# RMS factors of the MLP: a row in every partition by two transfers through DRAM, in place of four transposes and two copies

## The chip, the cores and the metric

One core of one Trainium2 chip runs the whole kernel. The metric is the device time of one execution in microseconds (us). The kernel before took 762.76 us (median of three runs, 762.75 to 763.80).

## The reference, cut to what matters

A decoder layer on 512 tokens of 1024 channels: a gated convolution and a sliding-window attention are merged and added to the residual `x`; then a squared-ReLU MLP; all float32. The change touches the first RMS norm of the MLP alone:

```python
def rmsnorm(x, g):
    y = x * lax.rsqrt(jnp.mean(x * x, axis=-1, keepdims=True) + EPS)
    return y * g
...
h2 = rmsnorm(x, mlp_norm_g)                                  # (512, 1024)
x = x + jnp.square(jax.nn.relu(h2 @ w_up)) @ w_down          # w_up (1024, 4096), w_down (4096, 1024)
return rmsnorm(x, final_norm_g)
```

The factor of a token is one positive number, so the kernel multiplies with it only after `w_up` and the ReLU: `relu(a * f) = relu(a) * f`.

## The kernel before, in words

There is no planner: each of the five engines has its own program, written out in the order in which it is to run, and the programs meet at semaphores. A wait stops everything behind it on its engine.

Twelve products of 1024 x 1024 weights follow each other as stages s = 0 to 11. Stages 0 to 3 belong to the mixers, and 4 to 11 are the MLP: an even stage multiplies with a quarter of `w_up`, the odd one after it with the same quarter of `w_down`. Each stage is done by a scheme of seven half-size products with sums of blocks (M1, N2, M6, M5, M7, M3, N4, in this order), and each of these in three passes over a high and a low part of both operands ("kinds" 0, 1 and 2 in `up_product`, L818, and `product`, L856). ACT rounds the high parts (`high_part` L1150 for weights, `s_high` L1166 and `h2_high` L1288 for activations); DVE subtracts to make the low parts (`low_part` L1694, `s_low` L1701, `h2_low` L1764) and does the sums. Weights come by the queues of SP (blocks, L485) and POOL (sums of blocks accumulated by the transfer: "T3" at L605, "T1" at L610 and L614).

In an even stage the output has channels in partitions and tokens along the free axis. So a token's factor must stand in every partition, as the row `rrow` [128, 512]. `relu(4, 0)` (L1859, instruction L1868) is the first to read it; fifteen later ones read it too.

How the row is made before: ACT's `square_part` (L1298) sums squares of the residual into `ss2`; DVE's `token_sums` (L1781) adds two halves; ACT takes the square root (L1359, after `high_part(4, M5)`); DVE's `token_factors` (L1785) takes the reciprocal into `rr2[:, 1, :]`, a factor a token, tokens in partitions, and copies it (L1789) to 128 columns each in `rbc`; PE transposes the four blocks of `rbc` (L809) into PSUM bank 7, between kind 0 and kind 1 of product M5 of stage 4; ACT copies the bank to `rrow` (L1368) after `copy_out(4, zc12, M6)`.

Behind `relu(4, 0)` on DVE stand `h2_low` of M3 and N4, `s_low(5, M1)`, `sum_t2(5)`, `low_part(4, M3)`, and on to stage 5. `square(4, 0)` on ACT (L1309) waits for `relu(4, 0)`, and behind it stand `s_high(5, M1)`, `high_part(4, M3)` and `copy_out(4, zc22, M5)` (L1202). Product M3 of stage 4 on PE waits for that copy (`copied`, L953).

Of the kernel before, what the change touches and what calls it, by code (L numbers as in the profile page):

```python
# [7 lines left out]
F32 = mybir.dt.float32  # L8
F32R = mybir.dt.float32r
ALU = mybir.AluOpType  # L10
ACT = mybir.ActivationFunctionType

P = 128
D = 1024
T = 512
KT = D // P
TB = T // P
# [20 lines left out]
M1, N2, M6, M5, M7, M3, N4 = range(7)  # L38
# [139 lines left out]
def build(nc, x, attn_norm_g, w_in, conv_w, w_conv_out, attn_sinks, rel_bias, w_attn_out, w_o,  # L178
          mlp_norm_g, w_up, w_down, final_norm_g, out):
    ctx = ExitStack()  # L180
    with ctx:
# [4 lines left out]
        def place(name, shape, dt=F32, offset=None):  # L186

            size = 4 * int(np.prod(shape[1:]))
            if offset is None:
                offset = top[0]  # L190
                top[0] = -(-(offset + size) // 64) * 64
            return nc.alloc_sbuf_tensor_at(name, shape, dt, offset=offset)
# [44 lines left out]
        tz = place("tz", [P, 2, T + 2])  # L237
        ty_at = top[0]
        ty = place("ty", [P, 2, T])
        rbc = place("rbc", [P, TB, P], offset=ty_at + 4 * T)  # L240
        zc11, zc12, zc22 = (place(n, [P, 4, 2 * P], offset=o) for n, o in
                            (("zc11", ta_at), ("zc12", tz_at), ("zc22", ty_at)))
        b2_sum, b1_sum = (place(n, [P, 4, 2 * P], offset=two_at + 6 * KT * T + o) for n, o in
# [49 lines left out]
        g1, g2 = 0, KT  # L293
        bias_rows = nc.dram_tensor("bias_rows", (HEADS, 3 * P), F32)
        h_sums = nc.dram_tensor("h_sums", (4, 2, P, 8 * P), F32)

        pair = [ctx.enter_context(nc.psum_tensor(f"pair{i}", [P, 2, T], F32)) for i in range(4)]
        bank = [pair[i // 2][:, i % 2, :] for i in range(8)]
# [7 lines left out]
        def sem(name):  # L306
            return ctx.enter_context(nc.semaphore(name))
# [28 lines left out]
        hs_in = [sem(f"hs_in{i}") for i in range(4)]  # L336
        rt_ready, h2_raw = sem("rt_ready"), sem("h2_raw")
        h2_sums, h2_split, h2_ready = sem("h2_sums"), sem("h2_split"), sem("h2_ready")
        ss2_ready, rr2_step, rbc_ready = sem("ss2_ready"), sem("rr2_step"), sem("rbc_ready")
        rrow_t, rrow_ready = sem("rrow_t"), sem("rrow_ready")  # L340
        b11_in, b22_in = sem("b11_in"), sem("b22_in")
        b12_in, b21_in = sem("b12_in"), sem("b21_in")
        m_hi, m_lo, t_sum = sem("m_hi"), sem("m_lo"), sem("t_sum")
# [286 lines left out]
        def _(pe):  # L630
# [170 lines left out]
                                                   res[:, 2 * i + b, 512 * j + k * P:512 * j + (k + 1) * P], ident[:, :])  # L801
                last.then_inc(rt_ready, 1)

            def row_transposes():

                pe.wait_ge(rbc_ready, 1)
                pe.wait_ge(h2_raw, 12)
                for b in range(TB):
                    last = nc.tensor.transpose(bank[7][:, b * P:(b + 1) * P], rbc[:, b, :], ident[:, :])  # L809
                last.then_inc(rrow_t, 1)  # L810

            def weight_parts(s, i):
                n = unit(s, i)
                thi = high[n % 2][:, :].rearrange("p (k n) -> p k n", k=4)
# [121 lines left out]
            for s in range(3, STAGES):  # L936
                if is_up(s):
                    g = up_no(s)
                    if s == 4:
                        pe.wait_ge(h2_raw, 8)  # L940
                    else:
                        pe.wait_ge(relu_done, 4 * ((s - 4) // 2))
                    up_product(s, M1, True, between=(1, corner_21) if s == 4 else None)
                    pe.wait_ge(drained, drained_before(s + 1))
                    up_product(s, N2, True)
                    pe.wait_ge(copied, 3 * g + 1)
                    up_product(s, M6, False)
                    if s == 4:
                        pe.wait_ge(h2_raw, 16)
                    up_product(s, M5, True, between=(0, row_transposes) if s == 4 else None)  # L950
                    pe.wait_ge(copied, 3 * g + 2)
                    up_product(s, M7, False)
                    pe.wait_ge(copied, 3 * g + 3)  # L953
                    up_product(s, M3, False)
                    pe.wait_ge(summed, 3 * g + 2)
                    up_product(s, N4, False)
                    continue
                base_ = drained_before(s)
                more = 1 if alone(s) else 0
                pe.wait_ge(summed, 3 * up_no(s - 1) + 1)  # L960
                product(s, M1, True)
                if s == 3:
                    pe.wait_ge(ao_copied, 1)
                if s == 5:
                    pe.wait_ge(rrow_ready, 1)
                product(s, N2, s < 6)
                pe.wait_ge(drained, base_ + 1)
                product(s, M6, False)
                if s == 3:
                    pe.wait_ge(mix_hi, 4)  # L970
                    pe.wait_ge(drained, 2)
                    residual_transposes(0, 0, 0)
                pe.wait_ge(summed, 3 * up_no(s - 1) + 3)
                product(s, M5, True)
                pe.wait_ge(drained, base_ + 2 + more)
                product(s, M7, False)
                pe.wait_ge(drained, base_ + 3 + more)
                product(s, M3, False)
                pe.wait_ge(drained, base_ + 4 + more)
                if s == 3:  # L980
                    pe.wait_ge(h2_raw, 4)
                    residual_transposes(1, 1, 0)
                product(s, N4, False, between=(2, corner_12) if s == 3 else None)
# [3 lines left out]
        def _(act):  # L987
# [300 lines left out]
            def h2_high(i):  # L1288
                src = {M1: h2_a11, N2: h2_a12, N4: h2_a22}.get(i, h2_sum[i])
                if i in (M1, N2, N4):  # L1290
                    act.wait_ge(h2_raw, {M1: 4, N2: 12, N4: 8}[i])
                else:
                    act.wait_ge(h2_sums, {M7: 1, M6: 2, M5: 3, M3: 4}[i])
                if i in (M5, M3):
                    act.wait_ge(h2_ready, {M5: M1, M3: N2}[i] + 1)
                a(h2_hi[i][:, :, :], src[:, :, :], ACT.Copy).then_inc(h2_split, 1)
# [44 lines left out]
            for s in range(4, STAGES, 2):  # L1341
                first = s == 4
                high_part(s, N2)
                if first:
                    square_part(4, 0, 1, 6)
                    square_part(5, 1, 1, 6)
                    raw_corner(3, h2_a21, 0, 2)
                high_part(s, M6)
                if first:
                    h2_high(M6)  # L1350
                copy_out(s, zc11, M1)
                if first:
                    square_part(6, 2, 0, 7)
                    square_part(7, 3, 0, 8)
                    h2_high(M5)
                high_part(s, M5)
                if first:
                    act.wait_ge(rr2_step, 1)
                    a(rr2[:, 0, :], ss2[:, 2, :], ACT.Sqrt, bias=eps[:, :], scale=1.0 / D).then_inc(rr2_step, 1)  # L1359
                if first:  # L1360
                    h2_high(M7)
                else:
                    square(s, 0)
                high_part(s, M7)
                copy_out(s, zc12, M6, -1.0)
                if first:
                    act.wait_ge(rrow_t, 1)
                    a(rrow[:, :], bank[7], ACT.Copy).then_inc(rrow_ready, 1)  # L1368
                    h2_high(M3)
                    h2_high(N4)  # L1370
                    square(s, 0)
                s_high(s + 1, M1)
                high_part(s, M3)
                copy_out(s, zc22, M5)
                high_part(s, N4)
                square(s, 1)
                high_part(s + 1, M1)
                square(s, 2)
                s_high(s + 1, N2)
                high_part(s + 1, N2)  # L1380
                square(s, 3)
                high_part(s + 1, M6)
                s_high(s + 1, M6)
                high_part(s + 1, M5)
                s_high(s + 1, M5)
                high_part(s + 1, M7)
                s_high(s + 1, M7)
                high_part(s + 1, M3)
                s_high(s + 1, M3)
                if s + 2 >= STAGES:  # L1390
                    act.wait_ge(s_lo, part_no(STAGES - 1, M5) + 1)
                    for b in range(2):
                        early_squares(b)
                high_part(s + 1, N4)
                s_high(s + 1, N4)
                if s + 2 < STAGES:
                    high_part(s + 2, M1)
# [37 lines left out]
        def _(dve):  # L1435
# [349 lines left out]
            def token_factors():  # L1785
                dve.wait_ge(rr2_step, 2)
                v.reciprocal(rr2[:, 1, :], rr2[:, 0, :]).then_inc(rr2_step, 1)
                dve.wait_ge(rr2_step, 3)
                v.tensor_copy(rbc[:, :, :], rr2[:, 1, :].rearrange("p (b n) -> p b n", n=1).to_broadcast([P, TB, P])  # L1789
                              ).then_inc(rbc_ready, 1)  # L1790

            def summed_to(s, z, i, j, part):

# [194 lines left out]
            h2_s3_s2()  # L1988
            h2_s1_s4()
            h2_low(M6)  # L1990
            low_part(4, M6)
            token_sums()
            h2_low(M5)
            token_factors()
            low_part(4, M5)
            sum_c11(4)
            h2_low(M7)
            low_part(4, M7)
            dve.wait_ge(rrow_ready, 1)
            relu(4, 0)  # L2000
            h2_low(M3)
            h2_low(N4)
# [118 lines left out]
```

## Time and profile before

| | us |
|---|---|
| median of three runs | 762.76 |
| the profiled execution | 763.45 |
| its span, first to last instruction | 761.7 |
| PE busy | 752.7 |
| DVE busy | 637.4 |
| ACT busy | 407.6 |

The profiled execution took 1.75 us more than its span. PE's matmuls are pipelined, so a row's length overlaps the next row by some tenths of a us; the distance between two starts is what a group of matmuls takes. On ACT and DVE too the next instruction starts about 0.1 us ahead of the end that is shown. The granted TensorE clock was 0.998 of full speed over the span, so it is the upper of its two levels (2.4 GHz) nearly everywhere.

### The profile page before, as it was taken

How to read it: one execution, taken by the hardware profiler on the slowest of the kernel's cores; microseconds unless marked ns; L12 is line 12 of the kernel's file. 1: busy time of each engine (PE TensorE's matmuls, PEld its weight loads, DVE VectorE, ACT ScalarE, POOL GpSimd, SP SyncE). 2: the span in 40 equal slices, each digit the busy share in tenths (PEclk: the TensorE clock that was granted, in tenths of full speed). 3: DMA queues.
4: the chain of work that ended last, by engine and by line, in shares of the span. 5: the costliest groups of instructions: out<-in, count | busy, mean ns of one | idle time of the engine just before them, and what ended most of it. 6: DMA issues, size and time to landing. Idle time of an engine off the chain costs nothing.

```text
span 761.7 us, 11518 instructions
## 1 busy us (share of the span) xinstructions
PE 752.7 (99%) x4563; PEld 675.0 (89%) x4563; DVE 637.4 (84%) x752; ACT 407.6 (54%) x529; POOL 75.9 (10%) x113
## 2 busy tenths in 40 slices
PE   8999999999999999999999999999999999999996
PEld 7888888888888999999988899889998999899985
DVE  5766688889896979886869899998799869986997
ACT  7424554453644655636616786654555356445565
POOL 3201000101112001010010101010101000010102
PEclk9999999999999999999999999999999999999999
DMA  7727313131219876779736866777676767777702
GB/s 255 244 83 278 111 55 111 56 111 55 72 39 262 242 186 169 194 237 327 235 80 198 219 160 173 174 205 177 175 209 172 215 166 190 196 184 203 194 1 111
DMA packets 70451, 128.13 MB, mean 168 GB/s; under 512 B 2620, under 2 KB 26244, under 8 KB 70404
## 3 DMA queue, kind: packets, MB, share of 16 engines
q1 hardware_dynamic: 53040, 85.23, 33.8%
q0 software_dynamic: 17152, 41.96, 25.4%
q8 instruction: 34, 0.56, 0.3%
q10 hardware_dynamic: 212, 0.28, 0.1%
q14 instruction: 13, 0.11, 0.0%
HBM read 121.14 MB, written 6.32 MB: 167 GB/s over the span
## 4 chain that ended last, share of the span: by engine, by line
PE 97%; DVE 1%; DMA 1%; ACT 0%; issue 0%; SPq 0%; ACTq 0%; DVEq 0%
PE pair L848 37%; PE pair L875 24%; PE pair L651 10%; PE pair L653 10%; PE pair L652 10%; PE pair L698 2%; PE pair L673 1%; PE pair L672 1%; PE pair L682 1%; DMA xn<-in_x 1%; PE pair L744 1%; PE pair L746 0%; PE pair L745 0%; PE pair L800 0%; DVE home_lo L1698 0%
## 5 line engine op out<-in xcount | busy, mean ns | idle before, releaser
L1164 ACT ACTIVATE high<-home_raw 128x2048 fp32r<-128x2048 f32 x84 | 160.9, 1916 | 156.2 <-PE pair L848 88.7
L1698 DVE TENSOR_TENSOR home_lo<-home_raw,high 128x2048 fp32r<-128x2048 f32 x84 | 192.2, 2288 | 35.3 <-ACT high L1164 34.7
L651 PE MATMUL pair<-h,wgt 128*128 128x512 f32 x320 | 126.7, 396 | 0.0
L653 PE MATMUL pair<-h,wgt 128*128 128x512 f32 x320 | 124.9, 390 | 0.0
L652 PE MATMUL pair<-h,wgt 128*128 128x512 f32 x320 | 124.8, 390 | 0.0
L653 PEld LDWEIGHTS pair<-h,wgt 128*128 128x128 f32 x320 | 60.1, 188 | 13.0
L652 PEld LDWEIGHTS pair<-h,wgt 128*128 128x128 f32 x320 | 60.3, 188 | 11.5
L651 PEld LDWEIGHTS pair<-h,wgt 128*128 128x128 f32 x320 | 60.2, 188 | 11.5
L875 PE MATMUL pair<-high,s_hi_tile 128*128 128x512 f32 x280 | 70.1, 391 | 0.0
L875 PE MATMUL pair<-home_lo,s_hi_tile 128*128 128x512 f32 x280 | 69.7, 390 | 0.0
L875 PE MATMUL pair<-high,s_lo_tile 128*128 128x512 f32 x280 | 69.7, 389 | 0.0
L875 PEld LDWEIGHTS pair<-high,s_lo_tile 128*128 128x128 f32 x280 | 52.6, 188 | 11.0
L875 PEld LDWEIGHTS pair<-home_lo,s_hi_tile 128*128 128x128 f32 x280 | 52.6, 188 | 10.9
L875 PEld LDWEIGHTS pair<-high,s_hi_tile 128*128 128x128 f32 x280 | 52.1, 188 | 10.5
L848 PE MATMUL pair<-h_hi,home_lo 128*128 128x256 f32 x448 | 58.4, 284 | 0.0
L848 PE MATMUL pair<-h_lo,high 128*128 128x256 f32 x448 | 58.4, 284 | 0.0
L848 PE MATMUL pair<-h_hi,high 128*128 128x256 f32 x448 | 58.3, 283 | 0.0
L848 PEld LDWEIGHTS pair<-h_hi,high 128*128 128x128 f32 x448 | 56.0, 192 | 0.3
L848 PEld LDWEIGHTS pair<-h_lo,high 128*128 128x128 f32 x448 | 55.7, 192 | 0.0
L848 PEld LDWEIGHTS pair<-h_hi,home_lo 128*128 128x128 f32 x448 | 55.7, 192 | 0.0
L1443 DVE TENSOR_TENSOR wgt<-raw,wgt 128x1024 fp32r<-128x1024 f32 x41 | 48.4, 1221 | 8.6 <-ACT wgt L1005 8.4
L1005 ACT ACTIVATE wgt<-raw 128x1024 fp32r<-128x1024 f32 x41 | 41.2, 1054 | 23.3 <-PE pair L653 23.1
(222 smaller groups left out, 1151.8 us busy)
## 6 DMA issues: line engine op xcount, KB each, us to landing
raw<-in_w_in SPq DMA_DIRECT2D x42, 512.0 KB, 4.8
home_raw<-in_w_up SPq DMA_DIRECT2D x16, 1024.0 KB, 5.5
home_raw<-in_w_down SPq DMA_DIRECT2D x16, 1024.0 KB, 5.1
home_raw<-in_w_up POOLq DMA_DIRECT2D x12, 1024.0 KB, 8.4
home_raw<-in_w_down POOLq DMA_DIRECT2D x12, 1024.0 KB, 8.5
home_raw<-in_w_conv_out SPq DMA_DIRECT2D x4, 1024.0 KB, 8.2
home_raw<-in_w_attn_out SPq DMA_DIRECT2D x4, 1024.0 KB, 5.2
home_raw<-in_w_in SPq DMA_DIRECT2D x4, 1024.0 KB, 5.4
```

Of the source, the lines that this page charges most:

```text
L651: mm(bank[j][:, :], wh, rhs[:, 0, k, :], start=(k == 0), stop=False)
L652: mm(bank[j][:, :], wh, rhs[:, 1, k, :], start=False, stop=False)
L653: last = mm(bank[j][:, :], wl, rhs[:, 0, k, :], start=False, stop=(k == KT - 1))
L672: mm(acc, q, khi[:, kg, keys], start=True, stop=False)
L673: last = mm(acc, q, klo[:, kg, keys], start=False, stop=True)
L698: last = mm(bank[B_PV][:, :], vs[:, kb, kg, :, :].rearrange("p a d -> p (a d)"), pt[:, part, kb, :], start=(e == 0), stop=(e == len(steps) ...
L848: last = mm(acc[:, f, :], w[:, k, f * P:(f + 1) * P], a_[:, k, :], start=(fresh and kind == 0 and k == 0 and f % 2 == 0), stop=(kind == 2 ...
L875: last = mm(pair[region(s, i)][:, b, :], a_[:, k, b * P:(b + 1) * P], w[:, k, :], start=(fresh and kind == 0 and k == 0), stop=(kind == 2 ...
L1005: a(wgt[weight_slot(s1)][:, 0, 1024 * e:1024 * e + 1024], raw[raw_slot(c1)][:, :], ACT.Copy).then_inc(hi_ready, 1)
L1164: a(high[n % 2][:, :], home_raw[home_of(s, name)][:, :], ACT.Copy).then_inc(m_hi, 1)
L1443: v.tensor_tensor(w[:, 1, 1024 * e:1024 * e + 1024], raw[raw_slot(2 * s1 + e)][:, :], f32(w[:, 0, 1024 * e:1024 * e + 1024]), ALU.subtract ...
L1698: v.tensor_tensor(home_lo[home][:, :], home_raw[home][:, :], f32(high[n % 2][:, :]), ALU.subtract).then_inc(m_lo, 1)
```

## The change

`rbc`, its copy, the four transposes and ACT's copy from PSUM are gone, with PE's waits for them. ACT instead issues two transfers on its own DMA queue: the first writes `rr2[:, 1, :]` (128 partitions of 4 factors) to a row of 512 in DRAM, 4 bytes at a time; the second reads that row of 2 KB into each of 128 partitions of `rrow`. ACT waits for the reciprocal ahead of the first, and for the landing of the first (`row_out`) ahead of the second. The square root stands ahead of `high_part(4, M5)` on ACT and no longer behind it; `token_sums` and `token_factors` stand around `low_part(4, M6)` on DVE, each one operation earlier than before. `relu(4, 0)` waits for the landing of the second transfer (`rrow_in`).

```diff
--- before.py
+++ after.py
@@ -237,7 +237,6 @@
         tz = place("tz", [P, 2, T + 2])
         ty_at = top[0]
         ty = place("ty", [P, 2, T])
-        rbc = place("rbc", [P, TB, P], offset=ty_at + 4 * T)
         zc11, zc12, zc22 = (place(n, [P, 4, 2 * P], offset=o) for n, o in
                             (("zc11", ta_at), ("zc12", tz_at), ("zc22", ty_at)))
         b2_sum, b1_sum = (place(n, [P, 4, 2 * P], offset=two_at + 6 * KT * T + o) for n, o in
@@ -293,6 +292,7 @@
         g1, g2 = 0, KT
         bias_rows = nc.dram_tensor("bias_rows", (HEADS, 3 * P), F32)
         h_sums = nc.dram_tensor("h_sums", (4, 2, P, 8 * P), F32)
+        factors_row = nc.dram_tensor("factors_row", (TB, P), F32)
 
         pair = [ctx.enter_context(nc.psum_tensor(f"pair{i}", [P, 2, T], F32)) for i in range(4)]
         bank = [pair[i // 2][:, i % 2, :] for i in range(8)]
@@ -336,8 +336,8 @@
         hs_in = [sem(f"hs_in{i}") for i in range(4)]
         rt_ready, h2_raw = sem("rt_ready"), sem("h2_raw")
         h2_sums, h2_split, h2_ready = sem("h2_sums"), sem("h2_split"), sem("h2_ready")
-        ss2_ready, rr2_step, rbc_ready = sem("ss2_ready"), sem("rr2_step"), sem("rbc_ready")
-        rrow_t, rrow_ready = sem("rrow_t"), sem("rrow_ready")
+        ss2_ready, rr2_step = sem("ss2_ready"), sem("rr2_step")
+        row_out, rrow_in = sem("row_out"), sem("rrow_in")
         b11_in, b22_in = sem("b11_in"), sem("b22_in")
         b12_in, b21_in = sem("b12_in"), sem("b21_in")
         m_hi, m_lo, t_sum = sem("m_hi"), sem("m_lo"), sem("t_sum")
@@ -801,14 +801,6 @@
                                                    res[:, 2 * i + b, 512 * j + k * P:512 * j + (k + 1) * P], ident[:, :])
                 last.then_inc(rt_ready, 1)
 
-            def row_transposes():
-
-                pe.wait_ge(rbc_ready, 1)
-                pe.wait_ge(h2_raw, 12)
-                for b in range(TB):
-                    last = nc.tensor.transpose(bank[7][:, b * P:(b + 1) * P], rbc[:, b, :], ident[:, :])
-                last.then_inc(rrow_t, 1)
-
             def weight_parts(s, i):
                 n = unit(s, i)
                 thi = high[n % 2][:, :].rearrange("p (k n) -> p k n", k=4)
@@ -947,7 +939,7 @@
                     up_product(s, M6, False)
                     if s == 4:
                         pe.wait_ge(h2_raw, 16)
-                    up_product(s, M5, True, between=(0, row_transposes) if s == 4 else None)
+                    up_product(s, M5, True)
                     pe.wait_ge(copied, 3 * g + 2)
                     up_product(s, M7, False)
                     pe.wait_ge(copied, 3 * g + 3)
@@ -961,8 +953,6 @@
                 product(s, M1, True)
                 if s == 3:
                     pe.wait_ge(ao_copied, 1)
-                if s == 5:
-                    pe.wait_ge(rrow_ready, 1)
                 product(s, N2, s < 6)
                 pe.wait_ge(drained, base_ + 1)
                 product(s, M6, False)
@@ -1353,19 +1343,22 @@
                     square_part(6, 2, 0, 7)
                     square_part(7, 3, 0, 8)
                     h2_high(M5)
+                    act.wait_ge(rr2_step, 1)
+                    a(rr2[:, 0, :], ss2[:, 2, :], ACT.Sqrt, bias=eps[:, :], scale=1.0 / D).then_inc(rr2_step, 1)
                 high_part(s, M5)
                 if first:
-                    act.wait_ge(rr2_step, 1)
-                    a(rr2[:, 0, :], ss2[:, 2, :], ACT.Sqrt, bias=eps[:, :], scale=1.0 / D).then_inc(rr2_step, 1)
-                if first:
+                    act.wait_ge(rr2_step, 3)
+                    with nc.allow_non_contiguous_dma("a factor a token"):
+                        act.dma_start(factors_row.rearrange("b p -> p b"), rr2[:, 1, :]).then_inc(row_out, 16)
                     h2_high(M7)
                 else:
                     square(s, 0)
                 high_part(s, M7)
+                if first:
+                    act.wait_ge(row_out, 16)
+                    act.dma_start(rrow[:, :], bass.AP(factors_row[:, :].tensor, 0, [[0, P], [1, T]])).then_inc(rrow_in, 16)
                 copy_out(s, zc12, M6, -1.0)
                 if first:
-                    act.wait_ge(rrow_t, 1)
-                    a(rrow[:, :], bank[7], ACT.Copy).then_inc(rrow_ready, 1)
                     h2_high(M3)
                     h2_high(N4)
                     square(s, 0)
@@ -1785,9 +1778,6 @@
             def token_factors():
                 dve.wait_ge(rr2_step, 2)
                 v.reciprocal(rr2[:, 1, :], rr2[:, 0, :]).then_inc(rr2_step, 1)
-                dve.wait_ge(rr2_step, 3)
-                v.tensor_copy(rbc[:, :, :], rr2[:, 1, :].rearrange("p (b n) -> p b n", n=1).to_broadcast([P, TB, P])
-                              ).then_inc(rbc_ready, 1)
 
             def summed_to(s, z, i, j, part):
 
@@ -1988,15 +1978,15 @@
             h2_s3_s2()
             h2_s1_s4()
             h2_low(M6)
+            token_sums()
             low_part(4, M6)
-            token_sums()
+            token_factors()
             h2_low(M5)
-            token_factors()
             low_part(4, M5)
             sum_c11(4)
             h2_low(M7)
             low_part(4, M7)
-            dve.wait_ge(rrow_ready, 1)
+            dve.wait_ge(rrow_in, 16)
             relu(4, 0)
             h2_low(M3)
             h2_low(N4)
```

## Rows read from the trace of the kernel before

**Rows 1.** page: busy time by engine; the ending chain by engine
```profile
PE 752.7 (99%) x4563; PEld 675.0 (89%) x4563; DVE 637.4 (84%) x752; ACT 407.6 (54%) x529; POOL 75.9 (10%) x113
...
PE 97%; DVE 1%; DMA 1%; ACT 0%; issue 0%; SPq 0%; ACTq 0%; DVEq 0%
```

**Rows 2.** chain of waits: start us, length us, engine, tile, line
```profile
460.65 0.44 PE pair L809 x4
```

**Rows 3.** timeline of PE: start us, length us, engine, line, operation, out<-in, count
```profile
460.49 0.60 PE L809 MATMUL pair<-ident,rbc 128*128 128x128 f32 x4
460.84 2.15 PE L848 MATMUL pair<-h_lo,high 128*128 128x256 f32 x16
...
464.75 2.08 PE L848 MATMUL pair<-h_hi,high 128*128 128x256 f32 x16
...
470.51 2.08 PE L848 MATMUL pair<-h_hi,high 128*128 128x256 f32 x16
...
498.38 1.98 PE L875 MATMUL pair<-high,s_hi_tile 128*128 128x512 f32 x8
```

**Rows 4.** timeline of ACT, same columns, in brackets idle before and its releaser
```profile
455.70 1.04 ACT L1296 ACTIVATE h_hi<-h_sum 128x1024 fp32r<-128x1024 f32 x1
458.83 1.92 ACT L1164 ACTIVATE high<-home_raw 128x2048 fp32r<-128x2048 f32 x1 [2.08 <-PE pair L848]
460.65 1.00 ACT L1202 ACTIVATE zc<-pair 128x1024 f32<-128x1024 f32 x1
461.55 0.59 ACT L1368 ACTIVATE rrow<-pair 128x512 f32<-128x512 f32 x1
...
464.75 1.06 ACT L1309 ACTIVATE hid<-zc 128x1024 f32<-128x1024 f32 x1 [0.72 <-DVE zc L1868]
...
468.62 1.01 ACT L1202 ACTIVATE zc<-pair 128x1024 f32<-128x1024 f32 x1
...
496.43 1.06 ACT L1189 ACTIVATE s_hi_tile<-m_sum 128x1024 fp32r<-128x1024 f32 x1 [1.31 <-DVE m_sum L1734]
```

**Rows 5.** timeline of DVE, same columns
```profile
452.87 2.29 DVE L1698 TENSOR_TENSOR home_lo<-home_raw,high 128x2048 fp32r<-128x2048 f32 x1
...
456.49 0.43 DVE L1789 COPY rbc<-rr 128x512 f32<-128x512 f32 x1
...
461.30 2.29 DVE L1698 TENSOR_TENSOR home_lo<-home_raw,high 128x2048 fp32r<-128x2048 f32 x1
463.50 1.22 DVE L1868 SCALAR_TENSOR_TENSOR zc<-zc,rrow 128x1024 f32<-128x1024 f32 x1
...
507.25 1.22 DVE L1705 TENSOR_TENSOR s_lo_tile<-hid,s_hi_tile 128x1024 fp32r<-128x1024 f32 x1 [0.66 <-ACT s_hi_tile L1189]
```

**Rows 6.** DMA issues: transfer, queue, count, KB each, median us from issue to landing
```profile
home_raw<-in_w_down SPq DMA_DIRECT2D x16, 1024.0 KB, 5.1
...
gfin<-in_final_norm_g SPq DMA_DIRECT2D x1, 512.0 KB, 6.9
out<-res ACTq DMA_DIRECT2D x1, 256.0 KB, 2.8
bias_rows<-ext SPq DMA_DIRECT2D x1, 24.0 KB, 3.9
...
rbt<-in_rel_bias POOLq DMA_DIRECT2D x1, 2.0 KB, 5.2
```

**Rows 7.** timeline of POOL: the transfer issued just ahead of the second new one
```profile
458.35 1.27 POOL L605 DMA_DIRECT2D home_raw<-in_w_down  x1 [22.57 <-DMA home_raw<-in_w_down]
```

**Rows 8.** busy time in 4 us stretches; last: granted clock, DMA share, GB/s
```profile
456.00:460.00 4.00, 4.00 (x35) 4.00 (x35) 3.96 (x5) 1.92 (x2) 1.27 (x1) 1.00 0.36 140
460.00:464.00 4.00, 4.00 (x36) 4.00 (x35) 4.00 (x4) 4.00 (x5) 0.00 (x0) 1.00 0.91 153
```

**Rows 9.** timeline of ACT's queue at the start: its own DMA issues
```profile
0.82 0.61 ACTq L1009 DMA_DIRECT2D prow<-in_attn_norm_g  x1
1.47 0.28 ACTq L1010 DMA_DIRECT2D prow<-in_mlp_norm_g  x1
```

## The prediction

> **What bounds the kernel now.** I read the page first: PE is busy for 752.7 us of a span of 761.7, and 97% of the chain that ended last is PE's [rows 1]. So a change outside PE costs or gains nothing until it makes PE wait, and one on PE counts in full. Then the chain in order of time: the four transposes that go are links of it, 0.44 us [rows 2]. Then the timelines of PE, ACT and DVE around them, to find how late the row `rrow` may come. PE has no idle time there. ACT waits 0.72 us for the first `relu` at 464.75 [rows 4]. DVE goes into `relu` at 463.50 straight from `low_part(4, M7)`, and its next idle time is the one of 0.66 us ahead of 507.25 [rows 5]: for 44 us DVE can't catch up what it loses.
>
> **What goes.** Four transposes: 0.35 us between the starts of the rows at 460.49 and 460.84, 0.44 us in the chain [rows 2, 3]. I take the 0.44. They are on the path, so the gain is 0.44 as long as PE never waits later. DVE's copy to `rbc`: it took from 456.49 to the next start at about 456.83, 0.34 us, ahead of `relu` [rows 5]. That lets DVE be ready for `relu` at 463.50 − 0.34 = 463.16; `low_part(4, M7)`, the operation ahead, reads what ACT ends at 458.83 + 1.92 = 460.75, so it can move from 461.30 to about 460.96 [rows 4, 5]. ACT's copy from PSUM, 0.59 us, was on the way to `relu`, and makes room for the second issue.
>
> **What moves.** `token_sums` goes ahead of `low_part(4, M6)`, which started at 452.87 [rows 5]; `token_factors` follows it at about 452.9 + 0.2 + 2.3 = 455.4 and is through at about 455.6. The root goes ahead of `high_part(4, M5)`; both still end where `h2_high(M7)` started, 455.70 [rows 4]. That is the first transfer's place, so ACT doesn't wait for the reciprocal, or by 0.1 us. These moves cost nothing: they lie under DVE's and ACT's work for products that PE reaches more than 2 us later.
>
> **The first transfer**, issued at about 455.7. Its issue holds ACT for something between the 0.28 and the 0.61 us of ACT's own DMA issues [rows 9]. `h2_high(M7)`, 1.04 us, comes behind it, and then ACT has 2.08 us of idle time until PE lets `high_part(4, M7)` start at 458.83 [rows 4]. So the issue is hidden, even at three times 0.61. With 512 pieces of 4 bytes it is unlike any other write here; the nearest rows are 2.8 us (256 KB stored by ACT's queue), 3.9 us (24 KB from SBUF to DRAM) and 5.2 us (a 2 KB table in pieces of 4 bytes, on POOL's queue) [rows 6]. The DMA engines are only 0.36 busy in these 4 us [rows 8]. I take 3.9, nearest in direction: it lands at 459.6. ACT asks for it after `high_part(4, M7)`, at 460.65 [rows 4], so up to 4.95 us cost nothing; at 5.2 us it holds ACT up by 0.25. `copy_out(4, zc12, M6)` stands behind this wait, and product M7 on PE needs it at 464.75 − 0.44 = 464.3 [rows 3]; with an issue of 0.4 ahead it ends at 460.65 + 0.4 + 1.0 = 462.05, which leaves 2.2 us more.
>
> The Trainium skill speaks against this transfer: "DMA: Bandwidth & Descriptors", section "Specifications", says that below 512 bytes a piece is read, changed and written back. No row here shows such a write, and the page gives no price for one; the 5.2 us row has small pieces on the other side only.
>
> **The second transfer**, issued at 460.65 with 256 KB in 128 pieces of 2 KB, is the term that decides. From below: 2.8 us, ACT's store of the same size on idle engines [rows 6]. From above: 6.9 us, the gain of the final norm spread over all partitions in the same manner, twice the size, behind another load [rows 6]. Between them: a load of 1 MB takes 5.1 us [rows 6], of which at some 400 GB/s 2.6 is moving; 2.5 remain for the way there and back, and 256 KB at that rate is 0.65: 3.15 us alone. But it isn't alone. POOL issued the accumulating T3 at 458.35 [rows 7], and from 460 to 464 the engines are 0.91 busy at 153 GB/s [rows 8]. With every second turn on each engine the 0.65 becomes 1.3 to 2. I take 4.2 us, as 2.5 + 1.7: landing at 464.85.
>
> **The sum.** `relu(4, 0)` starts at 464.9 where it was 463.50: 1.4 us late. ACT's chain behind it (square, `s_high`, `high_part(4, M3)`, `copy_out(4, zc22, M5)`) ended at 468.62 + 1.01 = 469.63, and product M3 needed that at 470.51 [rows 3, 4]. The room is 0.88 us, counted from PE's old schedule. The later tight place gives the same: `s_high` of M5 in stage 5 ended at 496.43 + 1.06 = 497.49, PE needed it at 498.38, room 0.89 [rows 3, 4]; the two are not added, since PE is late already when it gets there. So PE ends 1.4 − 0.88 = 0.5 us later than before: it gives up its 0.44 and waits 1.0 us in all ahead of M3. With 0.1 for the wake-ups of the chain I say +0.6 us. In general, with L the time from second issue to landing (and the first in time), the change is L − 3.6, and not less than −0.44.
>
> On the profiled execution's own time, 763.45 (span 761.7 and 1.75 around it), that is 764.05. That execution was 0.69 above the median of three, so on the median I say 762.76 + 0.6 = 763.4 us. What a measurement of this kernel can tell from no change is 0.2%, 1.53 us.
>
> **Rival 1: the transfer is hidden.** If L is 3.2 or less, `relu` starts by 463.9, PE never waits, and the gain of 0.44 stays: 762.3. For it: 2.8 us for a store of the same size, 3.15 alone. Against it: T3 on the same engines. The skill would say so too: by the fit in "DMA: Bandwidth & Descriptors", section "Anatomy of one DMA — SWDGE (gpsimd) path", about 2.0 us and the bytes at 436 GB/s, 256 KB take 2.6 us (its own estimate, of another queue kind), and the sum would be −0.44. The trace goes over that fit: it gives 4.4 us for 1 MB where the row has 5.1.
>
> **Rival 2: slower, the latency of DRAM takes the place of the transposes.** If L is above 5.1, or if the first transfer needs more than 4.95 us and the two add up to over 10.1, `relu` comes so late that PE's wait ahead of M3 grows past 2 us and the time rises by more than 1.53. With the 6.9 us row for the second it is 6.9 − 3.6 = +3.3: 766.1. With 5.2 for the first and 5.1 for the second it is +1.75: 764.5. With the four-byte writes at twice the 3.9 us row, 7.8, and 4.2 behind them, it is 2.85 + 0.6 = +3.45: 766.2. For it: the engines' load, and a kind of write that no row shows. Against it: 128 pieces are 8 an engine, and the first has idle engines.
>
> **Rival 3: the transfers hold up the weights.** T3 of stage 5 shares engines with the second transfer. By T3's issue at 458.35 [rows 7] plus a landing some 8 us later it is read only behind `relu` on DVE, which is late as well; I give it 0.3 us at most on the forecast: 763.7.
>
> **Chances.** Forecast (L from 3.2 to 5.1, −0.4 to +1.5, rival 3 in it) 0.45; rival 1 0.24; rival 2 0.31. Within 0.2%: 0.45 + 0.24, less 0.02 for an unseen gain and less 0.01 for forecasts that end just over: 0.66. Slower by over 0.2%: 0.32. Faster by over 0.2%: 0.02, since 0.44 us is all that goes from PE. The range goes from 762.0 (rival 1, and 0.3 for the spread of the runs) to 766.5 (both prices of rival 2 taken in).
>
> **What would show it.** In the changed profile: no transposes of `rbc`; the chain shorter by 0.44 around 460; DVE idle ahead of `relu(4, 0)`, from about 463.2 to 464.9, released by the transfer into `rrow`; PE waiting some 1.0 us around 470 ahead of product M3, and no further wait of PE to about 510; ACT without a long wait ahead of the second issue at about 460.7. The first transfer proves me wrong if ACT stands there for over 0.3 us, the second if it lands before 463.9 or after 465.8. The prediction as a whole is wrong if PE waits at another product, or if the clock granted to TensorE, 1.00 in both stretches (the upper level) [rows 8], falls in the new gap.

## The result, and the profile after

The changed kernel takes 775.88 us (median of 6 runs, 774.67 to 777.33) against 763.32 us (6 runs): the ratio is 1.0168, with a 95% interval of 1.0157 to 1.0179. It is 12.6 us slower. I had forecast 763.4 us, with a range to 766.5. The profiled execution took 775.38 us, its span is 773.7 us, 12.0 more than before; all that follows is told of that span.

The page of the changed kernel (busy time by engine, and the ending chain by engine), against [rows 1]:

```profile
PE 756.2 (98%) x4559; PEld 678.2 (88%) x4559; DVE 637.1 (82%) x751; ACT 407.2 (53%) x528; POOL 75.9 (10%) x113
...
PE 92%; DMA 3%; DVE 2%; ACT 2%; issue 1%; SPq 0%; ACTq 0%; DVEq 0%
```

PE is busy 3.5 us longer although four of its instructions are gone, and its share of the chain fell from 97 to 92%. DMA stands there with 3%. The chain in order of time (start us, length us, what) names the place:

```profile
455.24 11.08 DMA factors_row<-rr
466.34 8.22 DMA rrow<-factors_row
474.59 1.24 DVE zc L1858
```

19.3 us of two transfers, one after the other, where the transposes had been 0.44 [rows 2]. The transfers and the two engines around them, ACT first (start us, length us, engine or its queue, line, operation; in brackets the idle time ahead and its releaser), against [rows 4]:

```profile
455.24 0.42 ACTq L1352 DMA_DIRECT2D factors_row<-rr  x1
...
458.70 1.92 ACT L1154 ACTIVATE high<-home_raw 128x2048 fp32r<-128x2048 f32 x1 [1.93 <-PE pair L840]
466.34 0.37 ACTq L1359 DMA_DIRECT2D rrow<-factors_row  x1
466.81 1.02 ACT L1192 ACTIVATE zc<-pair 128x1024 f32<-128x1024 f32 x1 [6.20 <-DMA factors_row<-rr]
```

```profile
460.71 2.28 DVE L1691 TENSOR_TENSOR home_lo<-home_raw,high 128x2048 fp32r<-128x2048 f32 x1
474.59 1.23 DVE L1858 SCALAR_TENSOR_TENSOR zc<-zc,rrow 128x1024 f32<-128x1024 f32 x1 [11.60 <-DMA rrow<-factors_row]
```

ACT stands 6.20 us for the first landing, with `copy_out(4, zc12, M6)` behind it. DVE is through with `low_part(4, M7)` at 462.99, a little ahead of the forecast's 463.16, and then stands 11.60 us for the second landing; `relu(4, 0)` starts at 474.59 instead of 463.50 [rows 5]. PE, against [rows 3]:

```profile
462.28 2.08 PE L840 MATMUL pair<-h_hi,home_lo 128*128 128x256 f32 x16
467.89 3.43 PE L840 MATMUL pair<-h_hi,high 128*128 128x256 f32 x16 [3.54 <-ACT zc L1192]
471.16 2.08 PE L840 MATMUL pair<-h_lo,high 128*128 128x256 f32 x16
473.08 2.08 PE L840 MATMUL pair<-h_hi,home_lo 128*128 128x256 f32 x16
480.75 3.78 PE L840 MATMUL pair<-h_hi,high 128*128 128x256 f32 x16 [5.60 <-ACT zc L1192]
484.33 2.10 PE L840 MATMUL pair<-h_lo,high 128*128 128x256 f32 x16
```

PE waits twice, ahead of M7 and ahead of M3. And after each wait its first sixteen matmuls take longer: 3.27 us from 467.89 to 471.16 and 3.58 us from 480.75 to 484.33, where the passes around them take 1.92. The reason is in the columns on the right of the stretches (last three: granted clock, DMA share, GB/s), where both stretches of [rows 8] have a clock of 1.00:

```profile
460.00:464.00 4.00, 4.00 (x36) 4.00 (x35) 2.99 (x2) 0.61 (x1) 0.00 (x0) 1.00 0.13 11
464.00:468.00 4.00, 0.46 (x4) 0.26 (x3) 0.00 (x0) 1.19 (x2) 0.00 (x0) 0.92 0.53 55
468.00:472.00 4.00, 4.00 (x24) 4.00 (x25) 0.00 (x0) 1.73 (x2) 0.00 (x0) 0.66 0.98 210
...
480.00:484.00 4.00, 3.25 (x15) 3.25 (x16) 4.00 (x3) 2.50 (x2) 1.26 (x1) 0.50 0.15 39
```

The clock fell to its lower level (1.2 GHz, a granted 0.50) after PE had stood, 0.46 us busy from 464 to 468, and came back only while the next products ran.

**The account.** From 464.20, where M5 had ended, to 467.89: 3.69. From 475.00 to 480.75: 5.75. The slow passes: 1.35 and 1.66. Together 12.45, less the 0.44 of the transposes: 12.0, the difference of the spans.

What the DMA engines did from 454 to 474 us (first line: their busy share in tenths, 40 slices of 0.5 us; then issues with size and us to landing), and the packets of ACT's queue (q10) in the one us from 457:

```profile
DMA  5699999100000000131374334494399999999999
...
home_raw<-in_w_down POOLq DMA_DIRECT2D x1, 1024.0 KB, 16.8
home_raw<-in_w_down SPq DMA_DIRECT2D x1, 1024.0 KB, 12.6
rrow<-factors_row ACTq DMA_DIRECT2D x1, 256.0 KB, 8.2
factors_row<-rr ACTq DMA_DIRECT2D x1, 2.0 KB, 11.1
```

```profile
q10 hardware_dynamic: 528, 0.00, 29.7%
```

This is the main reading. The 512 pieces of 4 bytes (and 16 words for the semaphore) are out of the engines within that us. Then the sixteen engines show nothing until 462, and the landing is told at 466.3, 8.6 us after the last packet. T3, issued at 458.26, was moving from 460 on before (153 GB/s from 460 to 464 in [rows 8], 11 GB/s now); now its packets come after 462 and trickle, and it takes 16.8 us to land instead of 8.3. The block of weights that SP issued at 464.4 takes 12.6 instead of 5.1 [rows 6]. So the second transfer, issued at 466.34, comes upon both of them, and takes 8.2 us instead of the 4.2 that I had for it. It is its beginning that is late. The view of DMA from 466 to 470 has T3's queue alone; the first packets of ACT's queue come at 470.6, 4.3 us after the issue. In experiment 4 below they come 1.0 us after it (issue at 458.53). From first to last packet it is 3.4 us here and 3.6 there. ACT's queue in the changed kernel from 470 to 471, and in experiment 4 from 459 to 460:

```profile
q10 hardware_dynamic: 5, 0.01, 2.6%
...
q10 hardware_dynamic: 34, 0.07, 20.2%
```

### The profile page after: what moved, and what is told of

Its sections match the earlier page's. It is cut to its first block, busy times and chain, and to the rows that moved or that the text cites. A ratio compares the mean times of both kernels' runs of the same rounds, so it can differ in the third digit from the quotient of the medians.

```text
span 773.7 us, 11509 instructions
## 1 busy us (share of the span) xinstructions
PE 756.2 (98%) x4559; PEld 678.2 (88%) x4559; DVE 637.1 (82%) x751; ACT 407.2 (53%) x528; POOL 75.9 (10%) x113
## 4 chain that ended last, share of the span: by engine, by line
PE 92%; DMA 3%; DVE 2%; ACT 2%; issue 1%; SPq 0%; ACTq 0%; DVEq 0%
PE pair L840 33%; PE pair L867 24%; PE pair L651 9%; PE pair L653 9%; PE pair L652 9%; PE pair L698 2%; DMA factors_row<-rr 1%; DMA rrow<-factors_row 1%; PE pair L673 1%; PE pair L672 1%; PE pair L682 1%; DMA xn<-in_x 1%; PE pair L744 0%; PE pair L745 0%; PE pair L746 0%
## 5 line engine op out<-in xcount | busy, mean ns | idle before, releaser
L840 PE MATMUL pair<-h_hi,high 128*128 128x256 f32 x448 | 61.3, 292 | 9.1 <-ACT zc L1192 9.1
L840 PEld LDWEIGHTS pair<-h_hi,high 128*128 128x128 f32 x448 | 58.7, 201 | 9.9 <-ACT zc L1192 9.5
```

The lines of the kernel that those rows point to most:

```text
L840: last = mm(acc[:, f, :], w[:, k, f * P:(f + 1) * P], a_[:, k, :], start=(fresh and kind == 0 and k == 0 and f % 2 == 0), stop=(kind == 2 ...
```

## The experiments

The kernel before, run again beside them, took 762.94 us (19 runs, for experiments 1 to 3) and 763.05 us (27 runs, for 4 and 6).

**1. Who has to wait: both transfers issued by SP.**

```diff
-  act: wait rr2_step 3; dma factors_row <- rr2 ... wait row_out; dma rrow <- factors_row
+  sp, behind its second block of stage 5:
+      sp.wait_ge(rr2_step, 3); sp.dma_start(factors_row.rearrange("b p -> p b"), rr2[:, 1, :])
+      sp.wait_ge(row_out, 16); sp.dma_start(rrow[:, :], <the row to 128 partitions>)
```

> The changed kernel with both transfers issued by SP, so that ACT waits for neither; SP waits for the first landing behind its second block of stage 5. Theory A (only the landing of the row decides, ACT's wait of 6.2 us is hidden under it): the row lands when it did, near 474.6 us, product M7 of PE is no longer held up, PE waits ahead of M3 in one piece of some 10.7 us, and the time stays within 0.4% of the changed kernel's 775.9. Rival (ACT's blocked queue costs on its own): the time falls by the 3.7 us wait ahead of M7 and its slow 1.35 us behind, to 770 to 771.

Measured: 774.97 us (4 runs), ratio to before 1.0155 (1.0138 to 1.0172). The landings are 10.4 and 8.3 us. Waits of PE (total us, times, longest), then `relu(4, 0)` on DVE and the two passes of PE behind the wait:

```profile
PE pair L846 <- ACT zc L1198: 10.0, 1, 10.0
...
473.56 1.23 DVE L1858 SCALAR_TENSOR_TENSOR zc<-zc,rrow 128x1024 f32<-128x1024 f32 x1 [10.93 <-DMA rrow<-factors_row]
...
479.73 3.78 PE L846 MATMUL pair<-h_hi,high 128*128 128x256 f32 x16 [9.98 <-ACT zc L1198]
483.31 2.53 PE L846 MATMUL pair<-h_lo,high 128*128 128x256 f32 x16
```

One wait of 10.0 us in the place of two. The time is 0.9 us less than the changed kernel's, and the row came 1.0 us earlier (`relu(4, 0)` at 473.56). So ACT's blocked queue was hidden under the row's lateness: the 3.69 + 1.35 us at M7 are gone, and no more is won than the row's earlier landing gives. The rival's 770 to 771 us did not come. The time from issue to landing decides, whoever issues.

**2. The second transfer without the first** (`mlp_norm_g` is read in place of the factors).

```diff
-  act: wait rr2_step 3; dma factors_row <- rr2; wait row_out
   act.dma_start(rrow[:, :], bass.AP(
-      factors_row[:, :].tensor, 0, [[0, P], [1, T]]))
+      mlp_norm_g.tensor, 0, [[0, P], [1, T]]))
```

> The changed kernel without the first transfer and without the waits for the reciprocal and for its landing; the second reads 512 gains of the MLP norm in place of the factors, so the output is not the reference's. It prices the second transfer alone, issued at about 460.6. If its 8.2 us in the changed kernel came from the traffic that the first had held up (T3 and a block of weights both in flight with it), it lands after 4 to 5 us, and the time is 763 to 764.5, as my forecast's sum had it. If the broadcast of one row of DRAM is slow by itself, it lands after about 8 us, and the time is 3.6 under 8.2, near 767.9.

```profile
rrow<-in_mlp_norm_g ACTq DMA_DIRECT2D x1, 256.0 KB, 4.8
```

763.53 us (10 runs), ratio 1.0009 (0.9999 to 1.0018); landing after 4.8 us. So 3.4 of its 8.2 us came from what the first transfer had held up. T3 takes 10.4 us here, where it took 8.3 before: the second transfer slows it without any help of the first.

**3. The same 2 KB as 128 pieces of 16 bytes** (the tokens then stand in another order).

```diff
-factors_row = nc.dram_tensor("factors_row", (TB, P), F32)
+factors_row = nc.dram_tensor("factors_row", (P, TB), F32)
-act.dma_start(factors_row.rearrange("b p -> p b"), rr2[:, 1, :])
+act.dma_start(factors_row[:, :], rr2[:, 1, :])
```

> The changed kernel with the first transfer as 128 pieces of 16 bytes, one a partition; the row then holds the factors in another order of tokens, so the output is not the reference's. Theory A (each small write costs): the first lands after 4 to 5 us, before ACT asks for it at 460.6, T3 is no longer held up, the second transfer lands after 4 to 5, PE waits 1 to 2 us ahead of M3, and the time is 764 to 765. Theory B (other traffic): the first lands as late as before, near 11 us, and the time stays near 775.

```profile
rrow<-factors_row ACTq DMA_DIRECT2D x1, 256.0 KB, 5.0
...
factors_row<-rr ACTq DMA_DIRECT2D x1, 2.0 KB, 2.6
```

763.63 us (10 runs), ratio 1.0008 (0.9998 to 1.0018): all 12 us are gone, and the first lands after 2.6 us, earlier than either theory had it. T3's packets begin late here too, 4.7 us after its issue, but then it is the second transfer's packets that move ahead of them; in the changed kernel the engines stood idle. Size and number changed together here, so it doesn't say which of them it was.

**4. The same 512 pieces of 4 bytes, 64 bytes apart** (the second transfer reads gains, as in experiment 2).

```diff
-factors_row = nc.dram_tensor("factors_row", (TB, P), F32)
+factors_row = nc.dram_tensor("factors_row", (TB, P, 16), F32)
-act.dma_start(factors_row.rearrange("b p -> p b"), rr2[:, 1, :])
+act.dma_start(factors_row[:, :, 0].rearrange("b p -> p b"), rr2[:, 1, :])
```

> The changed kernel whose first transfer puts its 512 pieces of 4 bytes at 64 bytes from each other in DRAM; the second reads gains of the MLP norm in place of them, so the output is not the reference's. As many pieces of the same size as in the change, but no two in the same 64 bytes. Theory (pieces side by side disturb each other, not the number or size of them): the first lands after 3 to 4 us, T3 is moved at its usual pace (8 to 11 us to landing), the second lands after 5, and the time is 763 to 764.5. Rival (in the kernel the small writes are slow for the traffic around them, too): the time stays above 770.

```profile
rrow<-in_mlp_norm_g ACTq DMA_DIRECT2D x1, 256.0 KB, 4.9
...
factors_row<-rr ACTq DMA_DIRECT2D x1, 2.0 KB, 2.9
```

763.53 us (10 runs), ratio 1.0005 (0.9995 to 1.0014); T3 lands after 10.8 us. Number and size of the pieces are those of the change, and the first lands after 2.9 us instead of 11.1. This is the experiment that names the cause: pieces of 4 bytes side by side in DRAM.

**5. The small transfers by themselves.** Three runs of the kernel before with transfers of SP behind the last store, one at a time on idle engines.

```diff
 sp.wait_ge(out_done, 16 * 2 * TB)
+for dst, src in probes:
+    sp.dma_start(dst, src).then_inc(pr_sem[i], 16)
+    sp.wait_ge(pr_sem[i], 16)
```

> The kernel before, with ten small transfers of SP behind its last store, each issued when the one before has landed, so that the DMA engines are otherwise idle. The times of interest are the landings of these ten; the kernel's own time grows by their sum and is of no interest. In order: (1) 512 factors to a row in DRAM, 4 bytes a piece, as in the change; (2) the same again to the same place; (3) the same, but each piece 64 bytes from the next in DRAM; (4) 128 pieces of 16 bytes; (5) 4 pieces of 512 bytes; (6) one row of 2 KB from one partition; (7) 512 pieces of 4 bytes from DRAM into 128 partitions; (8) the row of 2 KB into each of 128 partitions; (9) 128 pieces of 4 bytes to DRAM; (10) 128 pieces of 4 bytes from SBUF into one partition of SBUF. Theory A (small writes into DRAM are slow by themselves, each piece a few tens of ns): (1) and (2) land after 9 to 12 us, (4) and (9) after 3.5 to 5, (5) and (6) after 2 to 2.5, (10) after about 2. Theory B (the changed kernel's 11.1 us came from the other traffic around it): (1) lands after 3 to 4 us. Theory C (pieces side by side disturb each other, sixteen of them in 64 bytes): (3) lands much earlier than (1), at 4 to 6 us, and (4) at 3 or so. Theory D (only the first touch of a fresh place in DRAM is slow): (2) lands after 3 and (1) after 11. The broadcast (8) lands after 3.1 us by the forecast's sum for idle engines.

> Again the kernel before with transfers of SP behind its last store, each issued when the one before has landed; the landings are of interest. In the first series 512 pieces of 4 bytes took 8.7 and 9.8 us side by side and 2.6 us at 64 bytes from each other, 128 pieces side by side 7.9 us, 128 pieces of 16 bytes 1.4 us. In order: (1) to (3) 512 pieces of 4 bytes at 8, 16 and 32 bytes from each other; (4) 256 pieces of 8 bytes side by side; (5) 128 pieces of 4 bytes at 64 bytes from each other; (6), (7), (8) 16, 32 and 128 pieces of 4 bytes side by side; (9) 512 pieces side by side. Theory A (writes into the same 64 bytes wait for each other, half a us each, and lines of 64 bytes run beside each other): 16, 8, 4 and 2 writes a line give some 8 us side by side, 4 to 5 at 8 bytes, 3 at 16 and 2.6 at 32; (4) with 8 writes a line 4 to 5; (5) about 2; (6), (7) and (8) are alike, 8 us each. Rival (writes into one row of 512 bytes wait for each other, about 60 ns each): (6) 16 pieces land after 2 to 2.5 us, (7) after 3 to 3.5, (8) after 8, and (1) to (3) fall with the number of pieces in 512 bytes, 64, 32 and 16: 5, 3.5 and 2.6 us. The two differ at (6) and (7).

> Once more the kernel before with transfers of SP behind its last store, one at a time, all in pieces of 4 bytes from a column of partitions to DRAM. So far: 16 pieces side by side landed after 1.3 us, 32 after 4.4, 128 after 9.2 and 7.9, four rows of 128 after 8.6 to 9.8, 128 pieces at 64 bytes from each other after 1.4. In order: (1) 32 side by side; (2) 32 as 2 runs of 16, the runs 4 KB apart; (3) 64 side by side; (4) 128 as 8 runs of 16, 4 KB apart; (5) 128 as 4 runs of 32, 4 KB apart; (6) 128 at 8 bytes from each other, 1 KB in all; (7) 128 side by side, each DMA engine's 8 pieces at 64 bytes from each other and so between those of the others; (8) 128 side by side in the order of the partitions; (9) the same again. Theory R (the writes into one stretch of some hundred bytes wait for each other, about 60 to 100 ns each, and stretches apart run beside each other): (1) 4.4, (2) 1.3 to 1.5, (3) 6, (4) 1.5, (5) 4.4, (6) 4 to 5, (7) to (9) 8 to 9. Theory N (what counts is how many pieces are in flight, wherever they go): (2) as (1), (4) and (5) as (8), but the 1.4 us for 128 pieces at 64 bytes speaks against it. Theory E (an engine's own pieces in one line disturb each other, the other engines' do not): (7) lands after 2 us or so where (8) takes 8 to 9, and (4), one piece an engine in each line, after 1.5.

Issues of the first run (name, queue, count, KB, us to landing): spaced by 64 bytes, in pieces of 16 bytes, and 128 side by side; the first two, side by side, landed after 8.7 and 9.8 us, and the broadcast after 3.2.

```profile
pr_c<-rr SPq DMA_DIRECT2D x1, 2.0 KB, 2.6
pr_d<-rr SPq DMA_DIRECT2D x1, 2.0 KB, 1.4
...
pr_f<-rr SPq DMA_DIRECT2D x1, 0.5 KB, 7.9
res<-rr SPq DMA_DIRECT2D x1, 0.5 KB, 2.0
```

Of the second run: 128 pieces of 4 bytes spaced by 64, then 16, 32 and 128 side by side:

```profile
pr_h<-rr SPq DMA_DIRECT2D x1, 0.5 KB, 1.4
pr_i<-rr SPq DMA_DIRECT2D x1, 0.1 KB, 1.3
pr_i<-rr SPq DMA_DIRECT2D x1, 0.1 KB, 4.4
pr_i<-rr SPq DMA_DIRECT2D x1, 0.5 KB, 9.2
```

Of the third: 32 side by side, 2 runs of 16 at 4 KB from each other, 64 side by side, 8 runs of 16, 4 runs of 32, and 128 in an order that puts the pieces of neighbouring partitions 64 bytes apart and fills the gaps with those of others:

```profile
pr_l<-rr SPq DMA_DIRECT2D x1, 0.1 KB, 3.0
pr_k<-rr SPq DMA_DIRECT2D x1, 0.1 KB, 1.8
pr_n<-rr SPq DMA_DIRECT2D x1, 0.2 KB, 6.8
pr_m<-rr SPq DMA_DIRECT2D x1, 0.5 KB, 6.5
pr_r<-rr SPq DMA_DIRECT2D x1, 0.5 KB, 6.4
...
pr_p<-rr SPq DMA_DIRECT2D x1, 0.5 KB, 7.2
```

All of them together, us to landing on idle engines:

| pieces | side by side | 8 bytes apart | 16 | 32 | 64 |
|---|---|---|---|---|---|
| 512 of 4 bytes | 8.6, 8.7, 9.8 | 4.4 | 2.8 | 2.3 | 2.6 |
| 128 of 4 bytes | 6.9, 7.9, 9.1, 9.2 | 3.4 | | | 1.4 |
| 64 of 4 bytes | 6.8 | | | | |
| 32 of 4 bytes | 3.0, 4.4 | | | | |
| 16 of 4 bytes | 1.3 | | | | |
| 256 of 8 bytes | 3.9 | | | | |
| 128 of 16 bytes | 1.4 | | | | |

Crowding (theory B) falls as the main cause: with nobody beside it the write takes 8.6 to 9.8 us, in the kernels 11.1 and 10.4. Of that difference 0.9 us is a later first packet, 1.8 us after the issue in the changed kernel and 0.9 alone. A cost for each piece (theory A of the first run) falls by 128 side by side, 7.9 us for a quarter of the pieces. The first touch of a place (theory D) falls: the second write to the same place took 9.8 us. What helps is distance, or 16 bytes in one piece. That the writes into 64 bytes wait for each other (theory A of the second run) falls by the 16 pieces side by side, 1.3 us; that stretches apart don't matter to each other (theory R, and the rival of the second run with its rows of 512 bytes) falls by the 8 runs of 16 at 4 KB from each other, 6.5 us, where it had 1.5. Only the distance of 4 KB was tried, so stretches at another distance stay open. Theory E, that only an engine's own pieces disturb each other, has the interleaved order (7.2) against it, as far as an engine takes eight neighbouring partitions; no trace here tells which engine moves which. The plain count (theory N) fits the 6.5 and 6.4 us, but not the 1.4 us at 64 bytes, nor the 1.8 for two runs of 16 where 32 side by side took 3.0 and 4.4. So what is shown is a rule of use: from some 64 pieces of 4 bytes side by side on, a write to DRAM lands after 7 to 10 us on idle engines, and 512 of them with 16 bytes between starts after 2.8. Why they wait for each other, and where, stays open.

**6. The repaired route with the right factors.** Pieces of 16 bytes, the row lands in another tile, and one copy of DVE puts the tokens in order:

```diff
+act.dma_start(rraw <- factors_row in (p, b) order, to 128 partitions)
+dve.wait_ge(rrow_in, 16)
+v.tensor_copy(rrow as "p b n", rraw as "p b n").then_inc(rrow_set, 1)
 relu(4, 0)
```

> A correct kernel on this route: factors go to DRAM as 128 pieces of 16 bytes, the row comes back with the four factors of a partition together, and DVE puts it in the order of the tokens with one copy (about 0.43 us) behind the landing. The run with such pieces and no copy was 763.63 and had relu at 463.6 by its own start; the copy adds 0.4 to 0.5 us to what PE waits: 763.9 to 764.4, that is 0.1 to 0.2% above the kernel before. If it is under 763.2, the row's lateness was not what kept the 0.44 us from showing.

763.48 us (11 runs), ratio to before 1.0006 (0.9997 to 1.0015). That is less than I had said: PE waited only 0.4 us ahead of M3, with `relu(4, 0)` at 463.80, and no longer ahead of M6 of stage 5 (see the end of the next section). And with the row's consumers moved back:

```diff
-relu(4, 0); h2_low(M3); h2_low(N4); s_low(5, M1); sum_t2(5); low_part(4, M3)
+h2_low(M3); h2_low(N4); <copy>; relu(4, 0); low_part(4, M3); s_low(5, M1); sum_t2(5)
-act: square(4, 0); s_high(5, M1); high_part(4, M3); copy_out(4, zc22, M5)
+act: high_part(4, M3); copy_out(4, zc22, M5); square(4, 0); s_high(5, M1)
```

> As the kernel with 16-byte pieces and a copy on DVE, and the consumers of the row moved back: on DVE the low parts of M3 and N4 come ahead of the row and low_part(4, M3) right behind relu(4, 0); on ACT high_part(4, M3) and the copy of M5's bank come ahead of square(4, 0). The row may then come 2.2 us later without an engine idle. If lateness of the row is all that stands against the 0.44 us taken from PE, the time is 762.3 to 762.7, 0.04 to 0.08% under the kernel before, which the intervals can hardly tell from none; PE has no wait between 455 and 510. If the second transfer costs PE in another way (weights late, T3 late), a wait of PE shows at those and the time stays at 763.3 or more.

```profile
463.87 1.22 DVE L1766 TENSOR_TENSOR h_lo<-h_a,h_hi 128x1024 fp32r<-128x1024 f32 x1
465.00 0.64 DVE L1998 COPY rrow<-rraw 128x512 f32<-128x512 f32 x1
465.67 1.22 DVE L1864 SCALAR_TENSOR_TENSOR zc<-zc,rrow 128x1024 f32<-128x1024 f32 x1
```

DVE goes into the copy, which took 0.64 us and not 0.43, without idle time, and PE has no wait around stage 4 and 5. 762.67 us (11 runs) against 763.05 (27 runs), ratio 0.9996 (0.9987 to 1.0005). That is the size of the 0.44 us, and the interval holds no difference: a version that beats the kernel before is not shown. The kernel before with only this order of the consumers was not run, so how much of the 0.4 us is the transposes' and how much the order's is open.

## Why the prediction was wrong

**The step that failed is the price of the first transfer.** I put 3.9 us, "nearest in direction", the row of 24 KB written from SBUF to DRAM, and called 5.2 us the upper row. It took 11.1. The rows that I had were of long pieces, or had the short pieces on the SBUF side (`rbt`, 5.2 us; in the first probe 512 such pieces read from DRAM took 2.1). I had written that this write is unlike any other in the trace, and then gave it the middle of three unlike rows; my highest price for it was twice 3.9. The honest upper bound was open. The sentence on the Trainium skill ("DMA: Bandwidth & Descriptors", section "Specifications", pieces below 512 bytes are read, changed and written back) pointed at the right transfer. But the price doesn't follow that size: 128 pieces of 16 bytes, far below 512, land after 1.4 us, and 512 of 4 bytes at 64 bytes apart after 2.6. Whether a small piece is read, changed and written back no run here shows.

**The second transfer was mis-sized for the same reason.** By itself its price came out: 3.15 us alone against 3.2 measured, and 4.2 beside T3 against 4.8 to 5.0 (experiments 2 to 4). That was luck, since the terms were off both ways. I had 2.5 us for the way there and back and 0.65 for the moving; in the first probe the packets began 1.1 us after the issue, took 1.8 and were told as landed 0.3 later. Beside T3 I had 2.5 and 1.7; in experiment 4 it was 1.0, 3.6 and 0.3. (The fit of the Trainium skill, "DMA: Bandwidth & Descriptors", section "Anatomy of one DMA — SWDGE (gpsimd) path", gave 2.6 us, an estimate; the trace has 3.2.) In the changed kernel it took 8.2, since T3 had not been moved when it was issued, and its first packets came 3.3 us later than in experiment 4. I had T3 slow the row, but not the row's write slow T3.

**A term was missing: the clock.** I named its fall as a thing that would prove me wrong, at no price. The two waits cost 3.0 us in slow passes. Of these 1.66, behind the wait ahead of M3, count on their own: by my own rule the change is (474.59 − 463.50) − 0.88 = 10.2, and with 1.66 it is 11.9 of the 12.0 us. The first wait and its slow pass lie under the row's lateness, as experiment 1 shows.

**The moves and the issue.** The copy's 0.34 us on DVE came out (ready at 462.99), the moves of the root and of `token_factors` cost nothing, and ACT didn't wait for the reciprocal. The second issue I had at 460.65, behind `high_part(4, M7)`. With a fast first transfer it goes out at 458.5 while that activation runs, for instance in experiment 4:

```profile
458.50 1.92 ACT L1154 ACTIVATE high<-home_raw 128x2048 fp32r<-128x2048 f32 x1 [1.93 <-PE pair L840]
458.53 0.37 ACTq L1359 DMA_DIRECT2D rrow<-in_mlp_norm_g  x1
```

So the issue went out 0.03 us after the activation ahead of it had started; it did not stand behind that activation's end, as I had counted. That gave the row 2.1 us which I had not counted, and the crowded transfer took back 0.7 of them.

**Rival 1** (hidden, −0.44) and my own forecast (+0.6) were sums for a first transfer that lands in time. Experiment 4 has such a one, and is 0.5 us above before, in an interval that holds both (−0.4 to +1.1). In it `relu(4, 0)` starts at 463.48, early enough for M3, and PE doesn't wait there. It does later (DVE, then PE):

```profile
463.48 1.23 DVE L1858 SCALAR_TENSOR_TENSOR zc<-zc,rrow 128x1024 f32<-128x1024 f32 x1 [0.68 <-DMA rrow<-in_mlp_norm_g]
...
468.88 2.29 DVE L1670 TENSOR_TENSOR home_raw<-home_raw,home_raw 128x2048 f32<-128x2048 f32 x1 [0.73 <-DMA home_raw<-in_w_down]
```

```profile
492.74 2.09 PE L867 MATMUL pair<-high,s_hi_tile 128*128 128x512 f32 x8 [0.41 <-DVE res L1739]
```

`sum_t2(5)` waits 0.73 us for T3, which took 10.8 us to landing, and PE waits 0.41 ahead of M6 of stage 5. That is **rival 3**, which I had allowed 0.3 us: about the whole gain. The last kernel of experiment 6 takes it away by putting `sum_t2(5)` later. **Rival 2** was the right one in kind (DRAM's latency takes the place of the transposes, decided at M3), at 0.31 and with prices to 766.2. Of the signs for my account, DVE idle ahead of `relu` and PE waiting ahead of M3 came true, both far longer than I had said. All the signs that I had named against it came true as well: ACT stood 6.20 us for the first transfer where 0.3 was the limit, the second landed at 474.6 where 465.8 was the latest, PE waited at another product, M7, which I had given 2.2 us of room after 460.65, and the granted clock fell.

## What to carry to other kernels

Before on-chip work of some tenths of a us is traded for a trip through DRAM, write down the latest time at which its result may come, and look for a row of the same kind of transfer: direction, size of a piece, distance of pieces. If there is none, its price is open upward, and a transfer put behind the kernel's last store measures it by itself: one form took 9 us, its neighbour 1.4. Where PE bounds a kernel, a late row can cost more than PE's wait: behind waits of 3.7 and 5.75 us here the granted clock was lower, while behind those of 0.4 us in experiments 4 and 6 it stayed at 1.00.

## What the runs showed of the hardware

- 512 words of 4 bytes, side by side in DRAM and written from 128 partitions, leave the DMA engines in under 1 us and are told as landed 7 to 9 us later (7.4 and 8.5 in the first probe, 8.6 in the changed kernel); at 16 bytes or more from each other the whole takes 2.3 to 2.8 us on idle engines.
- While such a write was pending, other queues stood too: T3's packets began 4.2 us after its issue instead of 2.0, with all engines idle, and then came at a fraction of their rate (44 GB/s from 462 to 468, 225 before; 16.8 us to landing instead of 8.3). The full rate came back at about 468.5, 2 us after the write had landed.
- 128 such words from SBUF into SBUF landed after 2.0 us (last row of the first probe) where 128 into DRAM took 6.9 to 9.2, so the slowness comes with DRAM as the target.
- TensorE's granted clock fell after PE's wait of 3.69 us (a mean of 0.66 from 468 to 472) and after that of 5.75 us (0.50 from 480 to 484); the pass of sixteen matmuls behind each, 1.92 us at the upper level, was 1.35 and 1.66 us longer. After the one wait of 10.0 us in experiment 1 two passes were, by 1.66 and 0.44 us.
